# Up-projections and index products placed around the state product of each chunk, and a relative bias sheared by 128 one-partition loads

## The reference, cut to what matters

```python
def step(state, xs):                                  # one chunk, every head
    q_c, k_c, u_c, w_c, g_c, a_c = xs
    v_new = u_c - w_c @ state
    o_c = (q_c * exp(g_c)) @ state + a_c @ v_new
    state = state * exp(g_last) + (k_c * exp(g_last - g_c)).T @ v_new
```

```python
idx_logits = einsum('bthd,bsd->bths', q_idx, k_idx)   # index products
score = einsum('bths,bth->bts', relu(idx_logits), w_idx)
_, sel = lax.top_k(score, topk)
bias = rel_bias[rel_bucket(t_pos - sel)]              # depends on the distance alone
logits = q @ k_sel * scale + bias
```

## Time and profile before

| | us |
|---|---|
| median of 3 runs | 1663.42 (1662.5 to 1663.88) |
| the profiled execution's own time | 1666.96 |
| its span | 1665.2 |
| PE busy | 1592.5 (96%) |
| DVE busy | 1310.6 (79%) |
| ACT busy | 701.9 (42%) |
| POOL busy | 585.0 (35%) |

### The profile page before, as it was taken

How to read it: one execution, slowest core, us unless ns; L and a number is a source line. 1 busy time by engine, 2 the same in 40 slices (tenths; PEclk the granted TensorE clock), 3 DMA queues, 4 the chain that set the end, 5 groups by cost and what they waited for, 6 DMA issues and landing times.

```text
span 1665.2 us, 26823 instructions
## 1 busy us (share of the span) xinstructions
PE 1592.5 (96%) x9293; PEld 1380.7 (83%) x9293; DVE 1310.6 (79%) x2405; ACT 701.9 (42%) x1118; POOL 585.0 (35%) x427
## 2 busy tenths in 40 slices
PE   7998788969999999999999999999999999999997
PEld 5876476547878999999999999998888888888886
DVE  6744466786733799999999999848988888888887
ACT  6574148254423343343354444433333333333334
POOL 2000026224510577887732333314333233322220
PEclk9999899869999999999999999999999999999999
DMA  4334610011233578888799999999999999999995
GB/s 144 102 96 39 21 41 27 0 39 51 89 102 135 156 231 280 289 273 291 257 300 355 341 348 343 345 323 411 384 381 387 389 380 389 387 363 344 355 364 197
DMA packets 149560, 405.77 MB, mean 244 GB/s; under 512 B 14144, under 2 KB 71744, under 8 KB 146016
## 3 DMA queue, kind: packets, MB, share of 16 engines
q1 hardware_dynamic: 109152, 245.23, 45.6%
q0 software_dynamic: 36864, 134.23, 21.2%
q10 hardware_dynamic: 3456, 25.17, 3.8%
HBM read 350.83 MB, written 53.74 MB: 243 GB/s over the span
## 4 chain that ended last, share of the span: by engine, by line
PE 56%; DVE 10%; issue 1%; ACT 0%; POOL 0%; DMA 0%; DVEq 0%; ACTq 0%
PE bank L1559 31%; PE bank L2088 7%; PE bank L2092 7%; PE bank L2089 7%; DVE own_waste L1873 3%; PE bank L2112 3%; DVE back L1924 1%; DVE rt_num L1895 1%; DVE rt_num L1888 1%; DVE rt_work L1889 1%; PE bank L2073 0%; DVE rt_pos L1917 0%; DVE rt_pos L1914 0%; DVE rt_cand L1907 0%; DVE rt_top L1916 0%
## 5 line engine op out<-in xcount | busy, mean ns | idle before, releaser
L1559 PE MATMUL bank<-rt_u_parts,rt_w_hi 128*128 128x512 f32 x1536 | 369.1, 389 | 0.0
L2088 PE MATMUL bank<-hi_parts,rt_u_parts 128*128 128x384 f32 x1024 | 350.7, 343 | 0.0
L2089 PE MATMUL bank<-lo_parts,rt_u_parts 128*128 128x384 f32 x1024 | 343.5, 335 | 0.0
L1559 PEld LDWEIGHTS bank<-rt_u_parts,rt_w_hi 128*128 128x128 f32 x1536 | 288.1, 188 | 59.8
L1788 ACT ACTIVATE rt_u_parts<-raw 128x1024 fp32r<-128x1024 f32 x126 | 133.8, 1062 | 337.3 <-PE bank L2092 302.5
L1425 ACT ACTIVATE rt_u_parts<-raw 128x1024 fp32r<-128x1024 f32 x128 | 135.9, 1062 | 319.6 <-PE bank L1559 300.4
L2141 POOL DMA_INDIRECT h<-u_rows_dram,own_experts x128 | 173.8, 1357 | 235.5 <-DVE own_waste L1873 221.6
L2147 POOL DMA_INDIRECT qy<-v_dram,own_experts x128 | 131.1, 1024 | 347.0 <-DVE qy L1499 341.1
L1481 DVE TENSOR_TENSOR rt_u_parts<-raw,rt_u_parts 128x1024 fp32r<-128x1024 f32 x128 | 156.7, 1224 | 66.0 <-ACT rt_u_parts L1425 65.6
L1835 POOL TENSOR_TENSOR rt_u_parts<-raw,rt_u_parts 128x1024 fp32r<-128x1024 f32 x66 | 162.9, 2468 | 123.9 <-ACT rt_u_parts L1788 122.8
L2092 PE MATMUL bank<-hi_parts,rt_u_parts 128*128 128x384 f32 x1024 | 199.2, 335 | 2.0 <-POOL rt_u_parts L1835 2.0
(11 more groups left out here) (356 smaller groups left out, 2405.1 us busy)
## 6 DMA issues: line engine op xcount, KB each, us to landing
raw<-u_dram SPq DMA_DIRECT2D x128, 512.0 KB
raw<-v_dram SPq DMA_DIRECT2D x128, 512.0 KB
active_scratch<-rt_act SPq DMA_DIRECT2D x128, 192.0 KB
gates_scratch<-front ACTq DMA_DIRECT2D x12, 1024.0 KB
gates_scratch<-back ACTq DMA_DIRECT2D x12, 1024.0 KB
front<-gates_scratch SPq DMA_DIRECT2D x8, 1536.0 KB
front<-active_scratch SPq DMA_DIRECT2D x64, 192.0 KB
back<-active_scratch SPq DMA_DIRECT2D x64, 192.0 KB
```

The lines of the kernel that those rows point to most:

```text
L1559: return mm(bank_of[b][z][:], left[:, b * P:(b + 1) * P], right[:, halves[z]], start=False, stop=stop)
L2088: mm(bank, u_hi[:, j % 2, chunk[c]], hi[:, c, 0:TD], start=c == 0, stop=False)
L2089: mm(bank, u_hi[:, j % 2, chunk[c]], lo[:, c, 0:TD], start=False, stop=False)
```

## The change

Two things are changed. First, in the chunk loop one group of PE work now stands between the state product and the wait for v_new: the four index products that stood behind the second product (n < 4), or an up-projection. The up-projections are spread by a table `UPS_AT` with keys (n, place): place 0 is ahead of the wait for v_new, place 1 behind the second product, place 2 behind the chunk's output. ACT's copies are put in the matching order. Second, the strip is written to DRAM once (4 by 640), from another buffer, and the bias is loaded by 128 transfers, one for each partition, of 4 rows of 512 elements.

```diff
+    UPS_AT = {(3, 2): range(0, 2), (4, 0): (2,), (4, 1): (3,), (4, 2): (4,), (5, 0): (5,), (5, 1): (6,), (5, 2): (7,),
+              (6, 0): (8,), (6, 1): (9,), (6, 2): (10,), (7, 0): (11,)}
-        buckets, strip = wide(mt_u, 0)[0:BUCKETS], wide(mt_u, 2)[0:H]
+        buckets, strip = wide(mt_u, 0)[0:BUCKETS], wide(sq, H)[0:H]
                 sp.wait_ge(s["strip_s"], 2)
-                for h in range(H):
-                    sp.dma_start(a_in["strip"][h:h + 1], strip[h:h + 1].unsqueeze(1).to_broadcast([1, P, W])).then_inc(s["strip_out"], 16)
+                sp.dma_start(a_in["strip"], strip).then_inc(s["strip_out"], 16)
...
-                sp.wait_ge(s["strip_out"], 16 * H)
+                sp.wait_ge(s["strip_out"], 16)
                 sp.wait_ge(s["w_t"], H)
-                for h in range(H):
-                    sheared = bass.AP(a_in["strip"].tensor, h * P * W + P - 1, [[W - 1, P], [1, T]])
-                    sp.dma_start(bias[:, h, :], sheared).then_inc(s["bias"], 16)
+                for p in range(P):
+                    sp.dma_start(bias[p:p + 1], a_in["strip"][:, P - 1 - p:P - 1 - p + T].unsqueeze(0)).then_inc(s["bias"], 16)
                 sp.wait_ge(s["wqi"], 16)
-                sp.wait_ge(s["bias"], 16 * H)
+                sp.wait_ge(s["bias"], 16 * P)
                 sp.wait_ge(s["up_out"], NUP)
...
-                dve.wait_ge(s["strip_out"], 16 * H)
...
-                        dve.wait_ge(s["bias"], 16 * H)
+                        dve.wait_ge(s["bias"], 16 * P)
...
                     last.then_inc(s["ws"], 1)
+                    if n < 4:
+                        for q in range(IH + 8 * n + 4, IH + 8 * n + 8):
+                            index_dots(q)
+                    for m in UPS_AT.get((n, 0), ()):
+                        up_project(NIDX + m)
                     pe.wait_ge(s["vnew"], n + 1)
...
                     last.then_inc(s["ds"], 1)
-                    if n < 4:
-                        for q in range(IH + 8 * n + 4, IH + 8 * n + 8):
-                            index_dots(q)
+                    for m in UPS_AT.get((n, 1), ()):
+                        up_project(NIDX + m)
...
-                    elif n < 7:
-                        if n == 3:
-                            pe.wait_ge(s["wq"], 16)
-                            pe.wait_ge(s["wkv"], 16)
-                            pe.wait_ge(s["latents"], 4)
-                        for m in range(3 * n - 9, 3 * n - 6):
-                            up_project(NIDX + m)
+                    if n == 3:
+                        pe.wait_ge(s["wq"], 16)
+                        pe.wait_ge(s["wkv"], 16)
+                        pe.wait_ge(s["latents"], 4)
+                    for m in UPS_AT.get((n, 2), ()):
+                        up_project(NIDX + m)
...
-    a["strip"] = nc.dram_tensor("strip_scratch", (H, P, T + P), F32).ap()
+    a["strip"] = nc.dram_tensor("strip_scratch", (H, T + P), F32).ap()
```

More of the change, by code:

```diff
@@ L1035, in _ @@
                         weighted(IH + 8 * n + 4, IH + 8 * n + 8)
+                    for part in range(2):
+                        for m in UPS_AT.get((n, part), ()):
+                            take_up(NIDX + m)
                     act.wait_ge(s["out"], n + 1)
@@ L1041, in _ @@
                         weighted(IH + 8 * n + 8, IH + 8 * n + 12)
-                    elif n < 7:
-                        for m in range(3 * n - 9, 3 * n - 6):
-                            take_up(NIDX + m)
+                    for m in UPS_AT.get((n, 2), ()):
+                        take_up(NIDX + m)
                 def log_of(h):
```

## The result

| | before | after |
|---|---|---|
| median beside each other | 1662.31 us (1656.58 to 1663.88, 7 runs) | 1649.9 us (1647.21 to 1653.26, 7 runs) |
| profiled execution, its own time | 1666.96 | 1647.21 |
| its span and mean granted clock | 1665.2, 0.979 | 1645.2, 0.990 |

The medians are 12.4 us apart. The ratio is 0.9939, with a 95% interval of 0.9921 to 0.9957, which is about 10 us. 1648.3 us was predicted, with a range of 1643.5 to 1657. The two profiled executions are 19.8 us apart, more than the 15.1 us of the sum and much more than the medians. Most of this part is about that difference.

The account below looks back on a forecast made before the run. PE, busy 96% of the span, was taken to bound the kernel. Strip 8.2 us plus loop 6.9 us made 15.1 us off, from a median of 1663.42 us to 1648.3 us; range 1643.5 to 1657.

Parts of the forecast that it names:

- The stop and its cause: PE's 5.62 us stop in the transposes near 181 us: instruction fetch stood behind the strip's slow packets.
- Strip term, 8.2 us: Writing the strip once removes PE's 5.62 us stop near 181 us and 2.58 us of slow products behind it.
- nothing else is due behind the stop: Near 181 us ACT and DVE only wait for PE, so no other work is late once the stop goes.
- Chunk 4's start, 3.4 us: Fewer up-projections ahead of state product 4 and earlier index products cut 3.4 of DVE's 4.01 us wait.
- Chunks 5 to 7, 4.5 us: With PE's wait for v_new filled, DVE's waits before chunks 5, 6 and 7 go, 4.51 us.
- the slow clock a separate risk of 1.0 us: Slow PE clock stretches in the chunk loop may return, losing up to 2 us; 1.0 us taken off.
- The prediction's 6.9: Whole chunk loop gain: 3.4 for chunk 4, plus 4.5 for chunks 5 to 7, less 1.0 for clock.
- 128 loads, cost 0: SP's bias loads during the loop, 0.46 us each, land in 62 us with 19 us to spare; cost nothing.
- PE doesn't keep up: Rival, 12%: slow stretches return or state product 4 stays late; half the loop's gain goes, 1651.7 us.
- The stop stays: Rival, 12%: PE's fetch near 181 us is late for another reason; only the loop's gain is left, 1656.5 us.
- Bias late: Rivals: loads delay the first logits by less than the gain (5%, 1655 us) or more (9%, 1698.6 us).

Follow-up runs that it names:

- e3: Kernel before with the strip in another buffer and its four slow writes issued only when the level stage begins: 1694.91 us, ratio 1.0214.
- e1: Kernel before with the chunk loop's new order alone, strip still written 128 times per head: 1652.6 us, ratio 0.9972.
- e12: Kernel before, unchanged, run again for another profile: 1660.12 us.
- e13: Kernel before, unchanged, run again for a second further profile: 1660.08 us.
- e2: Kernel before with the strip written once and the bias loaded by 128 one-partition transfers, old loop order: 1656.33 us, ratio 0.9987.
- e5: Changed kernel, unchanged, run again beside runs of before: 1650.5 us, ratio 0.9938.
- e11: Changed kernel with the index products of queries 16 to 19 moved into the last two levels of the inverse: 1648.69 us, ratio 0.9919.
- e4: Kernel before with two of the four slow strip writes, heads 2 and 3 taking the bias of heads 0 and 1: 1657.15 us, ratio 0.9986.
- e8: Changed kernel with 32 of the one-partition loads issued once more ahead of the 128, and one wait for them: 1666.67 us, ratio 1.0025.
- e10: Changed kernel with 56 additional loads of several shapes ahead of its 128, each group waited for: 1693.3 us, one run.
- e6: Changed kernel with the three up-projections of a chunk back behind its output, index products left ahead of v_new: 1658.32 us, ratio 0.9987.
- e7: Changed kernel with the index products back behind the second product, up-projections still spread: 1650.43 us, ratio 0.993.

## Why the prediction came out right, and which steps did not

**The stop and its cause: right.** The step "PE ran out of fetched instructions, and their fetch stood behind the slow packets of the strip" is borne out by e3: with the slow writes moved, the stops moved.

The Trainium skill (Runtime: NRT & Kernel Launch, section Instruction fetch mechanics) says that the crossing of a block is mostly hidden. The runs show when this holds: it is hidden with the block landing by 176 us in e1, e12 and e13, and not hidden at 5.6 us in the first profile and at 32 us in e3, though all five have the same four slow writes.

**Strip term, 8.2 us: mis-sized.** It is right for the profiled execution and wrong for the kernel. Two further profiles of before (e12, e13) have no stop, nor has e1 with the slow writes. By the medians of 12 executions of e2 and 29 of before the strip's change is worth 2.2 us, not clear of zero. The prediction gave the term two ends, 0 and 8.2, and took the upper one because of the row inside the stop; what it lacked was the question how often the stop comes. Of the 71 runs of before made beside the experiments and in the first comparison only 8 lie at 1666 us or above, where the profiled one lay. Whether these are the ones with the stop isn't known, as they have no profile.

The prediction also said that nothing else is due behind the stop, and that no engine's wait is put down to the write. That is so only with the stop. Without it DVE waits 0.5 to 1.5 us for the write's landing (e1, e12, e13), and that too goes with the change.

**Chunk 4's start, 3.4 us: near in size, only in part the order's doing.** The wait is 3.72 us in e12 and 0.72 and 0.74 in e5 and the changed kernel, so 3.0 us went, as was worked out for an ACT that doesn't run ahead. But PE's clock is 0.57 from 281 to 285 us in e12, ahead of this wait. e3 has the old order and a clock of 1.00 from 310 to 340 us. Its v_new of chunks 4 to 6:

```profile
327.40 0.68 DVE L892 TENSOR_TENSOR lo<-raw,bank 64x512 f32<-64x512 f32 x1 [2.80 <-PE bank L1280]
...
338.45 0.69 DVE L892 TENSOR_TENSOR lo<-raw,bank 64x512 f32<-64x512 f32 x1
...
350.26 0.68 DVE L892 TENSOR_TENSOR lo<-raw,bank 64x512 f32<-64x512 f32 x1 [2.08 <-PE bank L1280]
```

At the full clock the old order waits 2.8 us here, so the order is worth 2.1 us and the slow stretch of e12 another 0.9. The other way round, e11 has the order of the changed kernel at this place, a clock of 0.66 from 280 to 285 us, and a wait of 3.44 us. 1.7 of its 2.7 us above the changed kernel are the first up-projection, which takes 3.65 us instead of 1.96; 1.0 comes from a chunk 3 that begins earlier.

**Chunks 5 to 7, 4.5 us: wrong in its cause.** The step that failed is "DVE's waits before chunks 5, 6 and 7 (4.51 us) should go", reckoned as the order's doing, with the slow clock a separate risk of 1.0 us on the other side. 1.83 and 2.29 of these are the slow clock's doing: e12, e13 and e2 have the old order, a clock of 1.00 from 297 to 320 us, and only the 0.39 of chunk 6. In e3 and e4 a wait of 2.1 us stands before chunk 6, each time behind a slow stretch (a clock of 0.57 from 342 to 346 us in e3, 0.74 from 305 to 310 us in e4).

The loops of the old order are 80.2, 80.2 and 80.4 us in e12, e13 and e2, 82.0 in e3, 83.3 in e4 and 84.5 in the first profile. Those of the new order are 76.25, 76.29 and 76.3, and 77.5 in e8 and e10 up to the wait for the loads. In e3, e4, e8 and e10, 1.1 us of this is DVE's slow decay. Without it e3 is at 80.9, e4 at 82.2, and e8 and e10 at 76.4. So the new order is 4.0 us ahead at the clock of e12, and up to 8.2 where the clock was low more often. For a full clock throughout I estimate 3 us: 4.0 less the 0.9 of chunk 4's slow stretch is 3.1. From e3 it is 80.9 - 76.3 = 4.6, less the 1.7 us by which its wait before chunk 6 is longer than e12's 0.39, which is 2.9. No run shows it in one piece. The prediction's 6.9 came out between 4.0 and 8.2 by errors that partly cancel: 4.1 us too much for the order in chunks 5 to 7, and the clock with the wrong sign.

Whether the order keeps the clock up is open. In the five profiles of the changed kernel's loop (e1, e5, e8, e10, the changed kernel) the clock is 1.00 from 250 to 320 us, and all six profiles of the old order have a slow stretch ahead of chunk 7. PE waits 1.9 us for v_new in chunk 3 of the old order (e3, e4, e12), and at most 0.6 us there, for ACT, in the new. That speaks for it. Against it, e3 has the same wait without a slow stretch behind it, and e11 has a slow stretch behind a wait of 0.58.

**128 loads, cost 0: right, but by luck.** The step "one each 0.46 us" failed. It was 0.60, the nearest row being L2191 with 0.63, which the text had as its upper end. The spare was 1.7 us in the changed kernel, not 19, and e8 shows the price behind it: nearly the whole of each further us. The fixed cost of about 2.0 us that the prediction takes from the Trainium skill (DMA: Bandwidth & Descriptors, section Anatomy of one DMA) is given there for transfers issued from GpSimd, and SP issues these. e10's loads that were each waited for came round every 1.7 us.

**Rivals.** That PE doesn't keep up (1651.7) and the forecast (1648.3) both lie within the runs' spread; the measured 1649.9 stands between. The profiles decide for the forecast, since chunks 5 to 7 have no wait. "The stop stays" is out. "Bias late" is out by 1.7 us.

**How 12 us come about.** The closest pair in kind is e12 (1660.12 us) and e5 (1647.95).

- The level stage starts at 200.75 and 198.99 us, 1.8 us apart. 1.5 of them are the landing of the strip's write, the rest comes from the input stage.
- From there to the first v_new it is 54.1 and 52.15 us: 1.9 us, with a clock of 0.79 against 1.00 from 200 to 215 us.
- The loop is 80.2 and 76.3: 4.0 us, about 3 of them the order's by the estimate above.
- The eight products at its end take 5.62 and 3.70 us: 1.9 us. PE also begins them 9.5 us later in e12, when DVE's first logits are only 7.6 us later, behind a stretch of clock 0.58 from 325 to 330 us.
- By the expert stages (L2112, L2117) e5 is 828.91 - 817.78 = 11.1 us ahead, so 1.6 us more come behind the loop, and 1.1 us later still.

So the write and the order account for some 4.5 us. Nearly all of the rest that can be placed stands where e12's clock was lower. That the change causes this rest isn't shown: e6, e7, e8, e10 and e11 have no slow write and a clock of 0.69 to 0.77 from 200 to 205 us, and e1, with the new order, takes 6.36 us for the eight products.

**The whole.** The forecast took 15.1 us off, and the medians differ by 12.4. It took the strip at 8.2 us where e2 has 2.2, and the loop at 6.9 where e1 has 5.9. These two halves make 8.1 us by the medians, e5 has 10.3, and executions of one kernel scatter by more than the difference. The direction and most of the loop's part follow from the working. That the total came so near is partly luck.

## What to carry to other kernels

A wait for "issue" beside a landing packet of an instruction queue is real, and it moved when the slow transfers were moved (e3). But one profile shows one draw: before it goes into a sum at full price, ask what else could have made the landing early, and what waits next when it is. A wait for PE in a stretch of low clock belongs to the clock first; look at the same wait where the clock is full before crediting an order with it. For many small transfers take the dearest of the nearby issue rows, since the price hangs on the shape and a spare reckoned at 19 us can be one of 1.7.

## What the runs showed of the hardware

The mean granted clock and the span move together. For e5 span times clock is 1646.2 x 0.989 = 1628, for the changed kernel's first profile 1645.2 x 0.990 = 1629, for e6 1653.2 x 0.985 = 1628, for before 1658.1 x 0.983 = 1630 (e12) and 1665.2 x 0.979 = 1630 (the first profile). So nearly the whole difference between these executions, 20 us, is on record as clock. The product isn't a constant of all runs: over 64 runs of before it goes from 1628 to 1635, and e3 has 1649. Nor does it tell cause from effect, since a low clock also stands behind waits of PE: 0.68 in the stop of the earlier trace rows, and 0.50 from 184 to 192 us, before and behind its end.

Four transfers that each read one partition 128 times keep the queues 90% busy at 27 to 30 GB/s. The instruction block that lands by 160 us without them landed at 172 to 176 us with them in e1, e12 and e13 (and in e4, which has two of them), and at 184 to 185 in the first profile.

A load of 16 partitions with a wait behind it came round every 1.7 us, issue included ((25.81 - 0.31) / 15), where I had expected 2 to 3.
